# A hybrid decoder step on one core: mixing in two phases, output projection by token chunks, and both joined with the feed-forward

## The reference

```python
mix = sigmoid(parts[12]) * (o_nsa @ w_br_nsa) + sigmoid(parts[13]) * (o_hg @ w_br_hg)   # parts = h @ w_in
x = x + g1 * (mix @ w_out)
h2 = modulate(rms_norm(x, norm_ffn), sh2, sc2)                # g1, sh2, sc2, g2 = slices of c @ ada_w + ada_b
u, v = split(h2 @ w_up)                                       # D_FF = 2816 each
y = causal width-3 convolution of [buffer, u]
x = x + g2 * ((silu(y) * v) @ w_down)
```

## Time and profile before

| | us |
|---|---|
| median of the runs | 2386.66 |
| the profiled execution | 2395.94 |
| its span, first to last instruction | 2393.7 |
| busy: PE / PEld / DVE / ACT / POOL | 2206.7 / 1972.4 / 1163.5 / 629.4 / 581.5 |
| mixing, from its first to its last matmul | 1079.07 to 1430.2 |
| output projection, TensorE | 1442.75 to 1550.5 |
| feed-forward, first transposes; first product | 1558.31; 1572.66 |
| DMA over the span | 164.55 MB, 69 GB/s |

### The profile page before, as it was taken

One profiled execution on the slowest core, in us unless ns is written; L12 is line 12 of the kernel. 1 busy time (PEld: TensorE's weight loads), 2 busy tenths in 40 slices (PEclk: granted clock), 3 DMA queues, 4 the chain that ended last, 5 costly groups with the idle time before them and its releaser, 6 DMA issues. The chain is left out here.

```text
span 2393.7 us, 34630 instructions
## 1 busy us (share of the span) xinstructions
PE 2206.7 (92%) x13325; PEld 1972.4 (82%) x13325; DVE 1163.5 (49%) x2137; ACT 629.4 (26%) x1345; POOL 581.5 (24%) x354
## 2 busy tenths in 40 slices
PE   7999997998869999969999988979999999999996
PEld 3797785666646999968888978879999999999996
DVE  5763465888955267751111114164444534444444
ACT  3232464676732133320000011131101011101010
POOL 0112113445621255531001003122212112212120
PEclk9999897999979999969999999989999999999998
DMA  9021342000045322114324212022111111111101
GB/s 353 28 68 47 127 158 79 1 1 1 1 146 169 101 55 55 46 37 106 79 68 107 70 55 98 27 55 71 36 54 36 54 36 53 36 53 36 54 18 73
DMA packets 159568, 164.55 MB, mean 69 GB/s; under 512 B 9987, under 2 KB 139412, under 8 KB 154469
## 3 DMA queue, kind: packets, MB, share of 16 engines
q1 hardware_dynamic: 151446, 113.97, 16.0%
q0 software_dynamic: 7760, 48.55, 6.3%
q10 hardware_dynamic: 224, 0.08, 0.0%
HBM read 148.99 MB, written 17.87 MB: 70 GB/s over the span
## 5 line engine op out<-in xcount | busy, mean ns | idle before, releaser
L243 PE MATMUL psall<-hT_short,ring_short 128*128 128x344 f32 x1512 | 492.3, 326 | 31.6 <-issue 13.5
L245 PE MATMUL psall<-hT_short,ring_short 128*128 128x344 f32 x1512 | 487.3, 322 | 0.0
L238 POOL TENSOR_TENSOR ring_short<-ring,ring_short 128x2048 fp32r<-128x2048 f32 (+3 forms) x48 | 194.0, 4042 | 1068.7 <-DVE ring_short L233 1068.7
L244 PE MATMUL psall<-work_short,ring_short 128*128 128x344 f32 x1296 | 419.8, 324 | 0.0
L243 PEld LDWEIGHTS psall<-hT_short,ring_short 128*128 128x128 f32 x1512 | 288.6, 191 | 33.2 <-issue 26.6
L245 PEld LDWEIGHTS psall<-hT_short,ring_short 128*128 128x128 f32 x1512 | 288.2, 191 | 0.0
L244 PEld LDWEIGHTS psall<-work_short,ring_short 128*128 128x128 f32 x1296 | 248.6, 192 | 0.6
L2917 DVE SCALAR_TENSOR_TENSOR xT<-psall,mod,xT 128x344 f32<-128x344 f32 (+1 forms) x264 | 151.3, 573 | 129.6 <-PE psall L245 126.5
L2821 ACT ACTIVATE work<-psall 128x344 f32<-128x344 f32 (+1 forms) x66 | 30.0, 456 | 535.7 <-PE psall L245 535.6
L243 PE MATMUL psall<-work_short,work_short 128*128 128x344 f32 x480 | 160.9, 335 | 0.0
L244 PE MATMUL psall<-work_short,work_short 128*128 128x344 f32 x480 | 153.7, 320 | 0.0
(11 more groups left out here) (426 smaller groups left out, 4592.3 us busy)
## 6 DMA issues: line engine op xcount, KB each, us to landing
ring<-in_w_up SPq DMA_DIRECT2D x44, 512.0 KB, 5.0
ring<-in_ada_w SPq DMA_DIRECT2D x32, 512.0 KB, 3.8
work<-in_w_down SPq DMA_DIRECT2D x10, 1024.0 KB, 5.0
ring<-in_w_in SPq DMA_DIRECT2D x19, 512.0 KB, 4.6
work<-in_w_in SPq DMA_DIRECT2D x9, 512.0 KB, 5.0
x_spill<-xT SPq DMA_DIRECT2D x4, 1032.0 KB, 14.6
xT<-x_spill SPq DMA_DIRECT2D x1, 4128.0 KB, 15.2
ring<-in_ada_w SPq DMA_DIRECT2D x4, 1024.0 KB, 15.0
```

The lines of the kernel that those rows point to most:

```text
L238: return eng.tensor_tensor(lo, src, hi, ALU.subtract)
L243: pe.matmul(out, w[0], x[0], start=first, stop=False)
L244: pe.matmul(out, w[0], x[1], start=False, stop=False)
L245: return pe.matmul(out, w[1], x[0], start=False, stop=last)
```

## The change

Nothing is changed ahead of the mixing but loads: the recurrence stage now issues only the first gate weights ahead, not the branch weights. `stage_mix`, `stage_out_projection` and the class `Norm` go; `mix_programs` gives each engine a program that runs at the head of `stage_ffn`'s block, so two meetings of all engines go too.

- **Mixing.** All 48 gate chunks first (their sigmoids are kept, 16 tiles in `gate`), then all 48 branch chunks. Branch products are split: ACT casts the branch outputs `o` and the branch weights, DVE and POOL make the low parts. The 32 modulation panels go one after each set of three chunks, two more between the phases. Gate weights get their low parts from DVE. DVE multiplies, adds and makes the low part of the mix while the branches go on.
- **Output projection.** It goes over the eight tiles twice: chunks 0 and 1 first, then chunk 2, with the weights loaded twice (four buffers) and cut on ACT and POOL. `xT` comes back in four pieces during the branches.
- **Norm.** `SecondNorm` works in two parts (columns 0 to 687, and the rest). Squares are added up on DVE and POOL and TensorE sums once for each part. The scaling of part 0 lies beside the projection of chunk 2.
- **Feed-forward.** The transposes of the buffer's rows move into the projection, after its third tile. The first slice does four chunk products over columns of part 0, then chunk 2 of u and v over k. TensorE's loop is written out (`for g in range(1, GR)`); the loops of the other engines stay.

```diff
+    def collect(self, eng, p, n):                       # SecondNorm
+        eng.wait_ge(self.squared[p], n + 1)
+        wait(eng, self.collected[p], n - 1)
+        eng.tensor_tensor(self.acc[p], self.acc[p], self.sq[p][n % 2], ALU.add).then_inc(self.collected[p], 1)
...
+    def tensor(pe):                                     # mix_programs
+        for n in range(KT):
+            pe.wait_ge(gates.split, n + 1)
+            for b in range(2):
+                for c in range(3):
+                    wait(pe, opened, 6 * (n - 1) + 3 * b + c + 1)
+                    for k in range(KT):
+                        last = product(...)
+                    last.then_inc(gated, 1)
+                modulate(2 * n + b)
+        modulate(EARLY)
+        modulate(EARLY + 1)
+        for n in range(KT):
+            pe.wait_ge(branches.split, n + 1)
+            for b in range(2):
+                if n == 0:
+                    pe.wait_ge(opened, GATES - 6 + 3 * b + 3)
+                    for k in range(4):
+                        pe.wait_ge(o_split, 4 * b + k + 1)
...
+                else:
+                    for c in range(3):
+                        pe.wait_ge(weighed, 6 * (n - 1) + 3 * b + c + 1)
...
+                if EARLY + 2 + 2 * n + b < PANELS:
+                    modulate(EARLY + 2 + 2 * n + b)
+        for j in range(2 * KT):
+            pe.wait_ge(outs.split, j + 1)
...
+            for c in ((0, 1) if j < KT else (2,)) if j else ():
+                wait(pe, added, i - BANKS + 1)           # BANKS = 4
...
+            if j == KT:
+                pe.wait_ge(mod_read, 1)
+                norm.sum(pe, 0)
...
+    def scalar(act):                                    # second half of the projection
+        for n in range(KT):
+            act.wait_ge(added, 2 * KT + n + 1)
+            norm.square(act, 1, n)
+            if n + 11 < 2 * KT:
+                outs.take_high(act, n + 11)
+            if 2 <= n < 6:
+                norm.take_high(act, 0, 2 * n - 4)
+                norm.take_high(act, 0, 2 * n - 3)
...
+    def gpsimd(pool):
+        for n in range(KT - 1):
+            if n >= 1:
+                norm.collect(pool, 1, n)
+            if n + 11 < 2 * KT:
+                outs.take_low(pool, n + 11)
...
+    def vector(v):
+        for n in range(KT):
+            add(2 * KT + n, n, 2)
+            if n == 2:
+                v.wait_ge(norm.rstd_ready, 1)
+            if 2 <= n < 6:
+                for k in (2 * n - 4, 2 * n - 3):
+                    norm.scale(v, 0, k)
+                    if k:
+                        norm.take_low(v, 0, k - 1)
...
 def stage_ffn
+            mix.tensor(pe)
             pe.sem_inc(d_made, 1)
...
-            groups(pe, body)
+            body(0, 0, True, False)
+            for g in range(1, GR):
+                body(g, g % 2, True, True)
+            body(GR, 1, False, True)
```

More of the change, by code:

```diff
@@ L245, in product @@
     return pe.matmul(out, w[1], x[0], start=False, stop=last)
[L248 to L311, removed]
@@ L1921, in _ @@
             sp.wait_ge(projected, SLOTS * HGH)
[L1922 to L1924 removed]
+            next_weights.load(sp, 0)
         @block.gpsimd
@@ L2354, in __init__ @@
     def __init__(self, s, T):
[L2355 to L2358, removed]
+        self.raw = [view(s.ring, 4096 * i + 2048, 2, KT, P) for i in range(2)]
+        self.hi, self.lo = ([s.ring_short(4096 * i + at, 2, KT, P) for i in range(2)] for at in (0, 2048))
         self.loaded = [s.sem(f"x_loaded{i}") for i in range(2)]
@@ L2361, in __init__, with load, take_high, take_low @@
         self.w_in = T["w_in"][0].rearrange("(k p) n -> p k n", p=P)
+    def load(self, sp, n):
+        for branch, c in enumerate((C_GA, C_GB)):
+            sp.dma_start(self.raw[n % 2][:, branch], self.w_in[:, :, c + n * P:c + (n + 1) * P]).then_inc(self.loaded[n % 2], 16)
+    def take_high(self, v, n):
+        v.wait_ge(self.loaded[n % 2], 32 * (n // 2 + 1))
+        high(v, self.hi[n % 2], self.raw[n % 2]).then_inc(self.cut, 1)
+    def take_low(self, eng, n):
+        eng.wait_ge(self.cut, n + 1)
+        low(eng, self.lo[n % 2], self.raw[n % 2], self.hi[n % 2]).then_inc(self.split, 1)
@@ new lines, in load, with take_high @@
+    def load(self, sp, n):
+        raw, cols = self.raw[n % 2], slice(n * P, (n + 1) * P)
+        for dst, src in ((raw[0:HD, 0], self.nsa[0, :, :, cols]), (raw[HD:P, 0], self.nsa[1, :, :, cols]),
+                         (raw[:, 1], self.hg[:, :, cols])):
+            sp.dma_start(dst, src).then_inc(self.loaded[n % 2], 16)
+    def take_high(self, act, n):
+        act.wait_ge(self.loaded[n % 2], 48 * (n // 2 + 1))
+        act.activation(self.hi[n % 2], self.raw[n % 2], ACT.Copy).then_inc(self.cut, 1)
@@ L2483, in _ @@
-        @block.vector
-        def _(v):
-            ch = s.dve_chain
-            v.sem_inc(free_v, 3)
-            def cut_weights(h, times):
-                v.wait_ge(loaded[h], 80 * times)
-                high(v, w_hi[h], raw[h]).then_inc(cut, 1)
-            def body(n, h, i, more):
-                for branch in range(2):
+                            last = product(pe, s.ps[3 * b + c][:, 0:CH], (hi[:, b, k, :], lo[:, b, k, :]),
+                                           (o_hi[:, 4 * b + k, cols], o_lo[:, 4 * b + k, cols]), k == 0, k == 3)
@@ L2501, in body @@
-                        v.nop().then_inc(free_v, 1)
-                        if branch:
-                            v.tensor_tensor(at, at, part[:, cols], ALU.add)
-                if more:
-                    cut_weights(h, i + 2)
-            gate_weights.take_high(v, 1, 80)
-            with v.Fori(0, KT // 2 - 1) as i:
-                ch.enter(i, 12)
-                for h in range(2):
-                    body(2 * i + h, h, i, True)
-            ch.leave(KT // 2 - 1)
-            for h in range(2):
-                body(KT - 2 + h, h, 0, False)
@@ L2625 @@
+    mix = Core()
+    mix.sync, mix.gpsimd, mix.scalar, mix.tensor, mix.vector = sync, gpsimd, scalar, tensor, vector
+    mix.added, mix.banks_free, mix.rows_copied = added, MADE, rows_copied
+    return mix
 class UpWeights:
@@ L2723, in body @@
             def body(g, par, up, down):
-                if up:
+                if up and down:
                     low_up(2 * g + 1, 1)
```

609 lines of the change are left out of this document (367 added, 242 removed).

## The result

The changed kernel takes 2308.56 us (median of 4 runs, 2305.29 to 2309.33) against 2386.2 us for the kernel before on the same chip: a ratio of 0.9666 with a 95% interval of 0.9645 to 0.9686, so faster by 3.1 to 3.6%. The forecast was 2299 us in a range of 2284 to 2322. Direction, range and the places of the gain were right, while the median lies 1.6 us above the narrower forecast of 2293 to 2307. Of 87 us forecast, 78 came, and this part of the document says where a good half of the other nine are and what stays open.

The account below looks back on a forecast made before the run. TensorE, busy for 92% of the span, was taken to bound the kernel. 62 us from the changed part and 25 from the loop made 87, so 2395.9 became 2309, then 2299 us at the median, range 2284 to 2322.

Parts of the forecast that it names:

- Branch products: Mixing: each of 16 sets of 12 plain matmuls becomes 36 split ones, 7.02 to 5.65 us; 21.9 us less.
- Gates: Mixing's first phase: gate products with 16 modulation groups take 208.2 us, with 10 slow starts 209.5.
- the covers listed: Mixing: gate weights, branch start, branch weights with xT's return and the mix's lower halves all arrive in time, adding no wait.
- The two hand-overs: Around the projection: the 12.5 us hand-over goes wholly; the work of the 22.1 us one moves under other products.
- The price in the projection's second half: DVE and POOL exclude each other there: TensorE waits, a slow start and a late first feed-forward tile, 10 us, bounds 0 and 15.
- The changed part: From the first gate product to the end of the first feed-forward tile: 456.3 us against 518.4, 62 us less.
- The loop: Feed-forward: writing out TensorE's loop removes four jump gaps of 3.4 us with 2.9 slow start each, 25 us less.
- From the execution to the median: Whole kernel: the profiled execution lies 9.3 us above the median 2386.66, so 2309 us becomes 2299.
- A: Projection's second half: no DVE and POOL exclusion worth the name, 10 us more gain, 2289 us; chance 0.15.
- B: Feed-forward loop: the jump isn't the cause or the written-out stream stalls, so 25 us stay, 2324 us; chance 0.08.
- C: Hand-overs: more loss than 10 us, each further 3 us gap costing 6, 2311 to 2318 us; chance 0.19.
- D: Branch phase: loads starve it, making the kernel slower, 2392 us and up; chance 0.03.

Follow-up runs that it names:

- experiment 4: The changed kernel with plain fp32 branch products in place of split ones, their casts and differences gone too: 2330.27 us, ratio 0.9769.
- experiments 10: The changed kernel with one of the three modulation groups before the branches moved ahead of the last gate chunk: 2311.33 us, ratio 0.9684.
- experiment 11: The changed kernel with its last three modulation groups set one behind each of the last three gate chunks: 2309.83 us, ratio 0.9676.
- Experiment 5: The changed kernel without POOL's weight differences for the last five projection tiles, leaving out part of the result: 2300.74 us, ratio 0.9643.
- experiment 8: The changed kernel with the scaling of the first 688 columns moved back behind the projection: 2313.31 us, ratio 0.9699.
- experiment 1: The kernel before with only TensorE's feed-forward loop written out: 2365.83 us, ratio 0.9919.
- experiment 2: The changed kernel with TensorE's feed-forward loop put back, five turns of two groups: 2320.88 us, ratio 0.9728.
- 3: The changed kernel with a TensorE loop of two turns of four feed-forward groups, the rest written out: 2312.05 us, ratio 0.9698.
- 12: The changed kernel with the early gate cast, late projection differences on DVE and the last three modulation groups set singly: 2301.39 us, ratio 0.964.
- experiment 6: The changed kernel with the weight differences of the projection's last five tiles made by DVE, not POOL: 2308.26 us, ratio 0.9675.
- experiment 7: The changed kernel with DVE's first gate cast moved ahead of the last scaling of the recurrence output: 2306.71 us, ratio 0.9676.

## Why the prediction was right, and where its sizes were off

- **What bounds it.** Right: all that was gained lies where TensorE had less work or stood still; 82.1 us from the two stretches, 77.6 in the medians.
- **Branch products.** Forecast 21.9 less, measured 20.5 (experiment 4): I multiplied the pace by 36 and left out the first product behind each narrow group, 0.09 us more, 16 times.
- **Gates.** Forecast 209.5 for the products and 16 modulation groups, measured 211.4 (1069.07 to 1280.44). 16 times the same 0.09 is 1.4 of the 1.9. None of the covers listed failed: no wait in gates or branches, each quarter of xT back in 7.4 us, no wait for DMA. What the list missed was no wait at all: three narrow groups in a row, and 1.5 us of lower clock (experiments 10 and 11). In the earlier trace rows such groups stand alone, and in the row nothing shows what two in a row do.
- **The two hand-overs.** Right: both went, with their slow starts.
- **The price in the projection's second half.** Forecast 10 us: 5 of waits there, 2.9 of slow start, 2.4 at the end. The waits were 4.6, as placed, on POOL's weight difference for the last two products, and 1.9 at the end, 1.4 of it on the last scaled tile and square and 0.5 on ACT's copy of the first slice, which the forecast didn't have. The slow start did not come, in this execution; experiment 11 shows that it can. So 6.5 instead of 10. Experiment 5 shows the mechanism, exclusion between POOL and DVE, and experiment 8 that the overlap was worth 5.7 us all the same. The forecast's reading of the earlier trace rows was rough (6 x 1.12 and 6.13 make 12.9 of the 13.47 us): taken one by one, three of the six differences took 3.4 us each beside POOL and three 1.2 alone, which is the same exclusion. The Trainium skill, "SBUF — State Buffer", "Who interferes with whom", has a DVE operation with two SBUF inputs and a POOL one that reads SBUF exclude each other at a shared port pair; the trace agrees (0.92 us alone, 3.02 beside a POOL operation of 2.99).
- **The changed part.** Forecast 456.3 us. Gates 1.9 more, branches 1.4 and 1.5 more, waits 3.5 less make 457.6; measured 458.0. That the forecast lies within 2 us is thus in part luck: its terms missed by 4.8 one way and by 3.5 the other.
- **The loop.** Forecast 25, measured 21.7, and 21.9 alone in experiment 1. The mis-sized term is the slow start: I took the 22 slow matmuls behind the first gap for all four, while behind the other three it was about 12. The idle part, 3.4 on average, was right. The Trainium skill, "Runtime: NRT & Kernel Launch", "Instruction fetch mechanics", has a jump out of the prefetched window stall; the gaps agree, but one of the jumps of experiment 2 cost nothing.
- **From the execution to the median.** I took off the 9.3 us by which the profiled execution lay above its median. In kind that was right: its mixing began at 1079.07, and with the same code in experiment 1 at 1069.54. Of the 9.6 us between 2299 and 2308.6, the loop is 3.5 and the changed part 1.7; 0.6 is rounding, since the sum gives 2299.6. The last 3.8 I can't place: the start of the mixing varies by 10 us and the tail by 3 from one traced execution to the next, and medians of four are no sharper than that.
- **Rivals.** A fell by experiment 5, B by 1 and 3; C did not happen, since instead of further gaps there were shorter ones; of D the trace shows nothing.

## What to carry to other kernels

When a price is read off a repeated event, read all its occurrences; one windows answer over the four turns would have given 21.7 at once. Before an elementwise operation is moved beside POOL, sum the work that would exclude the other, and then compare with the place it would otherwise have: here up to three times the price under TensorE's cover was still better than the plain price in its path (5.7 us, experiment 8). And where the start of a stage scatters more than the effect sought, measure the stretch in the trace and let the median only confirm the sum.

## What the runs showed of the hardware

- TensorE's granted clock fell to the lower level with no idle time, in or just behind two or three groups of 16 fp32 matmuls of 9 columns in a row (3.5 to 5.5 us), in each of the ten kernels here that have them; it did not behind single groups (experiments 11 and 12, and the kernel before). What followed varied: mostly 11 wide matmuls, 1.5 us; in experiment 5, where it fell within the groups, 21 (2.8 us), and the groups themselves took 1.9 us longer.
- Behind the same wait of 2.85 to 2.90 us it fell once and stayed six times; behind one of 1.90 to 1.94 it fell once (experiment 6) and stayed twice; behind a gap of "issue" of 2.65 it stayed, and behind 3.1 to 3.6 it fell for 10 to some 20 matmuls. The cost of a gap is thus a range, not a number, and a short gap is no guarantee.
- A jump back in the feed-forward's long loop on TensorE cost 2.65 to 3.57 us of idle time in eight of nine cases; in the ninth it cost nothing, and no instruction block was fetched for that whole turn. The shorter loop of the mixing showed no gap at its turns.
- An 8-column DVE operation took 4.43 us instead of 0.17 for standing behind a POOL operation (experiment 7).
